# A hybrid decoder block with a PEER expert layer: swapping the operands of the second expert products, and moving the gate products from VectorE to GpSimd

## What is computed

```python
s = jnp.einsum("thpc,pkc->thpk", q, sub_keys)          # scores against 2 x 128 keys
...
expert_idx = jnp.take_along_axis(cand_i, pos, axis=-1)  # 16 experts per head, 8 heads, of 16384
gate = jax.nn.softmax(top_s, axis=-1)
u = u_tab[ib]
act = jax.nn.gelu(jnp.einsum("td,ted->te", xb, u), approximate=False)
return jnp.einsum("te,ted->td", act * gb, v_tab[ib])
```

## Time and profile before

| what | value |
|---|---|
| median of 3 executions | 2080.02 us (2073.47 to 2083.56) |
| profiled execution: its own time | 2084.04 us |
| profiled execution: span of the core | 2082.3 us |
| PE busy | 1965.2 us, 94% of the span |
| DVE busy | 1376.5 us, 66% |
| ACT busy | 815.7 us, 39% |
| POOL busy | 655.2 us, 31% |
| last stretch: first product of the second pass | 1519.53 us |
| last stretch: first add to `h` (L1865), last of eight ends | 2073.94 us, 2079.86 us |

### The profile page before, as it was taken

The page is one execution under the profiler, slowest core; times in us unless marked ns, Lnnn a source line. Parts: engine busy times, 40 slices in busy tenths (PEclk is TensorE's granted clock), DMA queues, the critical chain, the costliest instruction groups (busy, mean ns, idle before and its releaser), DMA issues. The chain is left out here.

```text
span 2082.3 us, 30616 instructions
## 1 busy us (share of the span) xinstructions
PE 1965.2 (94%) x11569; PEld 1751.7 (84%) x11569; DVE 1376.5 (66%) x2764; ACT 815.7 (39%) x1260; POOL 655.2 (31%) x682
## 2 busy tenths in 40 slices
PE   8999999999998799998998989999989999999999
PEld 7776677677666588898998979999989999999999
DVE  5542542532531564299899998888667787778777
ACT  4333433433432443242433336656533333333332
POOL 4133033032031100058987841322212222222221
PEclk9999999999998899999999999999999999999999
DMA  3210210210200642259997968888779999999997
GB/s 115 79 49 21 71 37 11 71 36 21 82 16 6 230 152 89 83 150 311 309 341 263 311 197 304 311 313 307 257 253 319 319 318 322 319 319 319 320 319 239
DMA packets 147986, 411.79 MB, mean 198 GB/s; under 512 B 15616, under 2 KB 63872, under 8 KB 147328
## 3 DMA queue, kind: packets, MB, share of 16 engines
q1 hardware_dynamic: 109056, 269.31, 37.4%
q0 software_dynamic: 38784, 140.53, 20.5%
HBM read 360.23 MB, written 49.55 MB: 197 GB/s over the span
## 5 line engine op out<-in xcount | busy, mean ns | idle before, releaser
L1417 ACT ACTIVATE expert_hi<-raw 128x1024 fp32r<-128x1024 f32 x288 | 305.4, 1061 | 423.9 <-PE psE L86 392.5
L84 PE MATMUL psE<-x2h,expert_hi 128*128 128x384 f32 x1024 | 349.5, 341 | 15.3 <-POOL expert_lo L1536 14.0
L84 PE MATMUL psE<-w_hi,expert_hi 128*128 128x384 f32 x1024 | 351.2, 343 | 10.3 <-DVE expert_lo L1572 5.7
L1572 DVE TENSOR_TENSOR expert_lo<-raw,expert_hi 128x1024 fp32r<-128x1024 f32 x215 | 263.0, 1224 | 148.2 <-ACT expert_hi L1417 147.2
L85 PE MATMUL psE<-x2l,expert_hi 128*128 128x384 f32 x1024 | 344.8, 337 | 0.0
L86 PE MATMUL psE<-x2h,expert_lo 128*128 128x384 f32 x1024 | 344.8, 337 | 0.0
L86 PE MATMUL psE<-w_hi,expert_lo 128*128 128x384 f32 x1024 | 344.0, 336 | 0.0
L85 PE MATMUL psE<-w_lo,expert_hi 128*128 128x384 f32 x1024 | 343.9, 336 | 0.0
L1530 POOL DMA_INDIRECT few_gathered<-in_peer_v,picked_expert x128 | 133.5, 1043 | 429.4 <-DVE few_y L1763 388.3
L1530 POOL DMA_INDIRECT few_gathered<-in_peer_u_rows,picked_expert x128 | 151.9, 1187 | 261.0 <-DVE few_gathered L1756 235.2
L1536 POOL TENSOR_TENSOR expert_lo<-raw,expert_hi 128x1024 fp32r<-128x1024 f32 x73 | 184.8, 2532 | 132.5 <-ACT expert_hi L1417 130.6
(11 more groups left out here) (295 smaller groups left out, 3521.2 us busy)
## 6 DMA issues: line engine op xcount, KB each, us to landing
raw<-in_peer_u SPq DMA_DIRECT2D x128, 512.0 KB
raw<-in_peer_v SPq DMA_DIRECT2D x128, 512.0 KB
expert_acts<-gelu SPq DMA_DIRECT2D x124, 192.0 KB
gelu<-expert_acts SPq DMA_DIRECT2D x124, 192.0 KB, 3.1
expert_gates<-shared SPq DMA_DIRECT2D x4, 4096.0 KB, 16.5
gates_in<-expert_gates SPq DMA_DIRECT2D x32, 512.0 KB
ring<-in_w_xonly SPq DMA_DIRECT2D x24, 512.0 KB, 3.3
ring<-in_w_full SPq DMA_DIRECT2D x16, 512.0 KB, 3.9
```

Of the source, the lines that this page charges most:

```text
L84: nc.tensor.matmul(out, sh, mh, start=first, stop=False)
L1417: nc.scalar.activation(wh[:, s % R, :], raw[:, s % R, :], ACT.Copy).then_inc(S["hi_done"], 1)
L1572: v.tensor_tensor(wl[:, s % R, :], raw[:, s % R, :], wh[:, s % R, :].bitcast(F32), ALU.subtract).then_inc(S["lo_done"], 1)
```

## The change

1. `outputs` swaps the operands. The weighted activations (`mh`, `ml`: 128 experts by 128 tokens) are the stationary operand and the expert rows (`wh`, `wl`) the moving one, 512 wide. The sums now have tokens on the partitions: 3 tiles of tokens by 2 halves of the width, 6 banks, 18 matmuls a chunk.
2. `h` is turned and put into those banks by TensorE at the start (`turn_h`, plain float32 matmuls with the identity, 4 for each bank, within chunk 0; 8 more for the first 128 tokens after it), so that the sums start from it. The 8 matmuls on `few_y` in the last chunk go.
3. `weigh` goes from VectorE to GpSimd, between the gathers. `low_w` waits for it as well.
4. The end: ScalarE and VectorE copy the halves of each tile out of PSUM, SyncE stores 6 halves and, before them, the tile of the first 128 tokens (`few_y` plus its turned `h`, one VectorE operation once the last row is used). The output has tokens as rows.

```diff
         @block.scalar
...
+            act.wait_ge(S["h_turned"], 2 * NT)
+            for t in range(NT - 1):
+                act.wait_ge(S["y_done"], 2 * t + 1)
+                nc.scalar.activation(out_rows[:, t + 1, 0:512], ps[:, OUT_BANKS[2 * t], :],
+                                     ACT.Copy).then_inc(S["first_taken"], 1)
         @block.gpsimd
...
+            def weigh(p):
+                j = chunk_at(p)
+                if p < R:
+                    pool.wait_ge(S["gelu_done"], j + 1)
+                else:
+                    pool.wait_ge(w_loaded[p % R], 16 * (p // R))
+                pool.wait_ge(gates_loaded[p // GATE_CHUNKS % 2], 16 * (p // GATE_CHUNKS // 2 + 1))
...
+                nc.gpsimd.tensor_tensor(part, part, gates_in[:, p // GATE_CHUNKS % 2, :, j % GATE_CHUNKS, :], ALU.mult)
+                part = acts[:, p % R, STORED:].rearrange("p (b t) -> p b t", t=BLOCK)
+                nc.gpsimd.tensor_tensor(part, part, kept[:, :, j, :], ALU.mult).then_inc(S["weighted"], 1)
...
-            for n in range(FIRST_DOTS, 2 * HK):
+            sent = FIRST_DOTS + R
+            for n in range(FIRST_DOTS, sent):
                 gather(n)
+            for p in range(N):
+                weigh(p)
+                while sent < min(few_upto(p - 2) + R, 2 * HK):
+                    gather(sent)
+                    sent += 1
         @block.vector
...
             def low_w(j):
+                dve.wait_ge(S["weighted"], j + 1)
                 dve.wait_ge(S["w_hi_done"], j + 1)
...
             for j in range(N):
-                if j + 2 < N:
-                    weigh(j + 2)
...
         @block.tensor
...
+            def turn_h(tile, half, bank):
+                for k in range(4):
+                    last = nc.tensor.matmul(ps[:, bank, k * P:(k + 1) * P], h[:, 4 * half + k, tile * P:(tile + 1) * P],
+                                            c["ident"][:, :], start=k == 0, stop=tile == 0 and k == 3,
+                                            skip_group_check=True)
+                last.then_inc(S["h_turned"], 1)
...
-                for m in range(DC):
...
-                    last = products(nc, ps[:, m, FEW:], (wh[:, j % R, cols], wl[:, j % R, cols]),
-                                    (mh[:, j % 2, :], ml[:, j % 2, :]), j == 0, j == N - 1)
...
+                for n, bank in enumerate(OUT_BANKS):
+                    t, half = divmod(n, 2)
...
+                        turn_h(t + 1, half, bank)
+                    tokens, cols = slice(t * P, (t + 1) * P), slice(half * 512, (half + 1) * 512)
+                    last = products(nc, ps[:, bank, :], (mh[:, j % 2, tokens], ml[:, j % 2, tokens]),
+                                    (wh[:, j % R, cols], wl[:, j % R, cols]), False, j == N - 1)
```

More of the change, by code:

```diff
@@ L83, in products @@
     (sh, sl), (mh, ml) = stationary, moving
-    nc.tensor.matmul(out, sh, mh, start=first, stop=False)
-    nc.tensor.matmul(out, sh, ml, start=False, stop=False)
-    return nc.tensor.matmul(out, sl, mh, start=False, stop=last)
+    nc.tensor.matmul(out, sh, mh, start=first, stop=False, skip_group_check=True)
+    nc.tensor.matmul(out, sh, ml, start=False, stop=False, skip_group_check=True)
+    return nc.tensor.matmul(out, sl, mh, start=False, stop=last, skip_group_check=True)
 def constants(nc, ctx, c):
@@ L1226 @@
 ROW_BANK = 0
+OUT_BANKS = (2, 3, 0, 1, 4, 5)
 TURN_BANK = 2
@@ L1862, in _ @@
                     low_w(j + 1)
-            for m in range(DC):
-                dve.wait_ge(S["y_done"], m + 1)
-                v.tensor_tensor(h[:, m, :], h[:, m, :], ps[:, m, :], ALU.add).then_inc(S["y_added"], 1)
+            dve.wait_ge(S["few_used"], 2 * HK)
+            dve.wait_ge(S["h_turned"], 2 * NT)
+            v.tensor_tensor(out_rows[:, 0, :], few_y, ps[:, 6:8, :].rearrange("p b d -> p (b d)"),
+                            ALU.add).then_inc(S["few_added"], 1)
+            for t in range(NT - 1):
+                dve.wait_ge(S["y_done"], 2 * t + 2)
+                v.tensor_copy(out_rows[:, t + 1, 512:], ps[:, OUT_BANKS[2 * t + 1], :]).then_inc(S["second_taken"], 1)
         @block.tensor
@@ L1965, in outputs @@
                 pe.wait_ge(S["w_lo_done"], j + 1)
[L1966 to L1973, removed]
-                    last = products(nc, ps[:, m, FEW:], (wh[:, j % R, cols], wl[:, j % R, cols]),
-                                    (mh[:, j % 2, :], ml[:, j % 2, :]), j == 0, j == N - 1)
+                for n, bank in enumerate(OUT_BANKS):
+                    t, half = divmod(n, 2)
+                    if j == 0:
+                        if bank == 0:
+                            pe.wait_ge(S["few_used"], FIRST_DOTS)
+                        if bank == 4:
+                            pe.wait_ge(S["gates_moved"], 2 * PAIRS_B)
+                        turn_h(t + 1, half, bank)
+                    tokens, cols = slice(t * P, (t + 1) * P), slice(half * 512, (half + 1) * 512)
+                    last = products(nc, ps[:, bank, :], (mh[:, j % 2, tokens], ml[:, j % 2, tokens]),
+                                    (wh[:, j % R, cols], wl[:, j % R, cols]), False, j == N - 1)
                     if j == N - 1:
[L1977 to L1980, removed]
+                        last.then_inc(S["y_done"], 1)
                 if j < N - 1:
                     last.then_inc(S["chunk_used"], 1)
+                if j == 0:
+                    pe.wait_ge(S["gelu_done"], N)
+                    for half in range(2):
+                        turn_h(0, half, 6 + half)
             for m in range(DC):
```

37 lines of the change are left out of this document (15 added, 22 removed).

## The result

| what | before | after |
|---|---|---|
| median of 3 executions | 2080.02 us | 2112.47 us (2109.18 to 2113.91) |
| ratio, 95% interval | | 1.0163 [1.0132, 1.0195] |
| profiled execution: its own time, span | 2084.0, 2082.3 us | 2109.2, 2107.5 us |
| PE, DVE, ACT, POOL busy | 1965.2, 1376.5, 815.7, 655.2 us | 1967.9, 1370.7, 817.0, 930.5 us |

The kernel is 1.6% slower, +32.5 us by the medians. The forecast was 2133.6. GpSimd has gained 275.3 us of busy time, and VectorE has lost only 5.8, although about 0.7 us of work in each of 128 chunks, some 90 us, has left it. In the second pass alone VectorE is even busier than before, 442.5 us for 438.6: its rows have grown by about what it gave away.

The account below looks back on a forecast made before the run. The prediction took a 4.22 us chain over ScalarE and VectorE, nearly balanced with TensorE, to bound the second products at 4.32 a chunk. Loop +48.8 and turning `h` +4.8 made +53.6 on 2080.0: 2133.6 us, range 2086 to 2150.

Parts of the forecast that it names:

- both halves blocking `low`: Second products: VectorE's `low` waits for both GpSimd halves of `weigh`; loop 4.73 us, 2133.6 us; chance 0.44.
- the first rival: Second products: engines take turns between `weigh`'s halves (4.57 us, 2114) or GpSimd is quicker (4.38, 2092); chance 0.32.
- The bound before: Second products: a 4.22 us chain over ScalarE and VectorE plus one chunk on TensorE, halved, gives 4.32 a chunk.
- Operands swapped: Second products: 18 matmuls 512 wide for 24 of 384, loop 4.28 without anything else, -0.04 us a chunk.
- `weigh` off VectorE gives nothing: Second products: `weigh` was covered by VectorE's wait for ScalarE, outside the chain, so removing it alone gains nothing.
- Where the two engines meet: Second products: `weigh` runs F + 1.30 to F + 2.44; `low` asks inside it, at F + 1.3 to F + 1.8.
- I take it that `low` waits for both: Second products: VectorE does not get in between `weigh`'s halves; loop 4.73 us, +48.8 us over 120 chunks.
- Turning `h`: Chunk 0: 32 float32 matmuls on TensorE's path, +7.2 us; eight on `few_y` go at the end, -2.4; net +4.8.
- the last store and copies at zero: End of the kernel: last copy about as long as the last sum, last store again 256 KB; zero, bounds 0.5.
- The sum: Whole kernel: 48.8 for the loop plus 4.8 for turning `h`, +53.6 us.
- The Trainium skill's two rules: Second products: gather not held up by `tensor_tensor`, loop 4.53, +29.6; GpSimd sum 1.96 times slower, about 4.93, +77.6.
- The 0.20: Second products: how much sooner the gather would end if `tensor_tensor` did not hold up descriptor generation; loop 4.53.

Follow-up runs that it names:

- swap_only: The change with `weigh` left on VectorE, against the kernel before: 2080.73 us, ratio 1.0013.
- pool_128: The change with only the 128-element half of `weigh` on GpSimd, the other on VectorE, against the kernel before: 2080.00 us, ratio 0.9998.
- pool_fill: `swap_only` plus two GpSimd memsets of an unused tile behind each gather, in place of `weigh`; against the kernel before: 2080.56 us, ratio 1.0015.
- early_w_swap: `swap_only` with `split_w` ahead of `hi` and `low_w` ahead of `low` and `few_next`; against the kernel before: 2049.65 us, ratio 0.9863.

## Why the prediction was right, and where it was off

The change costs time, for the reason given: the two engines meet where the forecast put them. The time forecast rests on a case that did not occur, both halves blocking `low` (chance 0.44, 2120 to 2145); 2112.47 lies in the case of the first rival (0.32, 2090 to 2120). That this rival's 2114 comes within 2 us of it is in part luck: its +34.4 stands against +37.4 in the second pass, and the rest is made up ahead of it.

- **The bound before (beat 4.32, chain of 4.22 with TensorE).** Right. Taking `low` and `few_next` out of the chain gives 4.16 with 24 matmuls and 4.08 with 18, TensorE's own pace in both. (The `hi` that waits for the end of a chunk is that of four chunks later; "two" in the text is the distance to the product that the chain holds up.)
- **Operands swapped, -0.04 a chunk, -5 us with the loop otherwise the same.** `swap_only` has a mean beat of 4.321 for 4.351, -0.03: its gaps are 518.5 us for 522.1, -3.6, and the stretch with the turning is 23.9 for 18.8, +5.1. So it comes out level (1.0013), as these terms would have it.
- **`weigh` off VectorE gives nothing.** Right for the half that could be tried alone: `pool_128` takes it off and adds no wait, and is level (0.9998); its gaps are 519.0 us, `swap_only`'s 518.5.
- **Where the two engines meet.** Right: with F the end of `few_next`, `weigh` starts at F + 1.34 (F + 1.30 in the text), and `low` asks inside its first half, at F + 1.57. The direction and its cause follow from this, and `pool_fill` shows that without GpSimd's reads nothing is lost.
- **"I take it that `low` waits for both", a loop of 4.73, +48.8 us.** This is the step that failed. `low` waits for the first half only and is served before the second, though no semaphore stands between the halves; `few_next` waits for the second. The loop is 4.58, and the 120 gaps cost 31.2 us. The evidence for the choice, VectorE standing 2.92 us past four GpSimd operations, was a true row but not a rule for this pair; the turns at 1203.75 in the same group were the better one. The rival's own sum (0.27 + 1.01 + 0.02 + 0.72 - 0.13 + 1.14 + 0.08 - 0.14 + 0.45 - 0.13 + 1.28 = 4.57) meets the rows link by link within 0.07: the gather takes 1.05 for 1.01 and the first half 0.75 for 0.72, but `few_next` ends 1.08 after the second half for 1.15, so that the differences nearly cancel (4.59 in the chunk shown).
- **Turning `h` +7.2, end -2.4, net +4.8.** Measured +6.7 in the stretch with the turning. Behind the gaps it is -1.3 to the last matmul and +0.8 from there to the end, together -0.5 for -2.4. The net is +6.2. The forecast had the last store and copies at zero with bounds of 0.5; they cost 0.8. The last of the copies ends 2103.35 + 0.69 = 2104.04, 1.1 after the start of the last matmul (2102.93).
- **The sum.** 31.2 + 6.2 = 37.4 in the second pass, against 53.6; the medians say 32.5. The 5 us between lie in the first stretch. Over the twelve profiles of this study the second pass begins between 1504.6 and 1519.7 us after the span's start, the two of the change at 1506.7 and 1513.0, the two of before at 1519.5 and 1517.7. I put the difference down to that spread; whether a part of it is the change's stays open.
- **The Trainium skill's two rules.** The Trainium skill, "SBUF — State Buffer", section "Who interferes with whom", has it that `tensor_tensor` does not hold up the generation of descriptors. The traces do not agree for a gather begun inside such an operation: in the kernel before, the one at 1092.23 lasted 2.81 and ended 0.81 after the `tensor_tensor` of the earlier trace rows; which part of a gather stands still is not shown. The gathers of the change take 1.05 for the 0.81 that the forecast took by that rule. So its loop of 4.53 is not how the loop closes, although +29.6 lies close to what was measured. The 0.20 was mis-sized as well: a gather that no two-input operation holds up takes 0.94 (below), so without that wait it would end 0.07 sooner than the 1.01 of the earlier trace rows, and the loop would be 4.66. The Trainium skill, "GPSIMD Engine Reference", section "Elementwise — side-by-side cycle accounting", has the ratio of 1.96 for 2048 elements. For these sizes it is too high: 0.75 against 0.42 for 256 elements is 1.8, 0.47 against 0.28 for 128 is 1.7.

## What to carry over

In this kernel an elementwise operation moved to GpSimd was free only where it was over when VectorE's next operation with two SBUF inputs asked (0.07 us of overlap cost nothing); what reached further was paid by VectorE, inside the durations of its own rows. Before moving work off an engine, look for the chain and for the order in it: here two short operations stood behind two long ones that nobody waited for so soon, and putting them first gave 1.4% with the swapped operands (0.9863, the best of all that ran), while moving work between engines gave nothing at best. A gain on TensorE that hardly shows (the swap) may only be hidden behind such a chain.

## What the hardware showed that I had not expected

- Two GpSimd operations in a row, with no wait between them, let a waiting VectorE operation in between: `low` ends 1.09 after the first of them (1907.21 to 1906.12), and the second lasts 1.47 for 0.47. Yet in the first stage one VectorE operation stood past four such, 2.91 to 2.92 us in all twelve profiles. What tells the two cases apart was not tried.
- The wait is booked as busy time on both engines: the second half alone has (1.42 - 0.47) x 119 = 113 us of it on GpSimd, of the 275 us by which it grew.
- A memset on GpSimd under VectorE's `low` costs it nothing (1.23), nor does an operation of GpSimd that reads SBUF cost one of VectorE that takes its second input from PSUM (1.22).
- In these traces a gather is held up by a two-input operation that VectorE has begun before it, not by one begun after. With `low_w` begun before it, it takes 1.01 to 1.05; with `low_w` begun inside it, in `early_w_swap`, 0.94:

```profile
1800.81 0.94 POOL L1542 DMA_INDIRECT few_gathered<-in_peer_v,picked_expert  x1 [3.14 <-DVE few_y L1775]
1801.20 0.56 DVE L1813 TENSOR_TENSOR w_lo<-gelu,w_hi 128x384 fp32r<-128x384 f32 x1 [0.65 <-ACT w_hi L1478]
```
